# A hybrid decoder step on one core: head norms summed in two column groups, roots by Ln and Exp, halves carried by DMA

## The reference, cut to what matters

```python
def rmsnorm(x, g):
    return x * rsqrt(mean(x * x) + EPS) * g                  # over D_MODEL = 1024
def group_rmsnorm(o, g):
    return o * rsqrt(mean(o * o over one head) + EPS) * g    # over 128 features of one head

n = rmsnorm(x, ln1)
rq, rk, rv, rg, gq, gk, gv, gg, ga, m_r, m_g = split_cols(n @ w_in)
o_r = retention of rotary(rq), rotary(rk), rv                # 4 heads, dk 128, dv 128
y_r = (group_rmsnorm(o_r, g_ret) * silu(rg)) @ w_ret_out
o_g = gated linear attention of gq, gk, gv, ga               # 4 heads, dk 64, dv 128
y_g = (group_rmsnorm(o_g, g_gla) * silu(gg)) @ w_gla_out
x = x + (sigmoid(m_r) * y_r + sigmoid(m_g) * y_g) @ w_o
...                                                          # rmsnorm ln2, ConvFFN of width 2816, final norm
```

## Time and profile before

| | us |
|---|---|
| median of three runs | 824.88 |
| lowest, highest | 824.02, 825.15 |
| the profiled execution | 826.43 |
| span of its trace (first to last instruction) | 824.60 |
| mean granted clock of PE | 0.997 of full speed |

### The profile page before, as it was taken

How to read it: one execution, slowest core, us unless ns; L and a number is a source line. 1 busy time by engine, 2 the same in 40 slices (tenths; PEclk the granted TensorE clock), 3 DMA queues, 4 the chain that set the end, 5 groups by cost and what they waited for, 6 DMA issues and landing times.

```text
span 824.6 us, 15722 instructions
## 1 busy us (share of the span) xinstructions
PE 815.2 (99%) x6528; PEld 801.7 (97%) x6528; DVE 587.9 (71%) x765; ACT 376.4 (46%) x528; POOL 217.0 (26%) x258
## 2 busy tenths in 40 slices
PE   9999999999999999999999999999999999999996
PEld 9999999999989999999999999999999999999996
DVE  4465768487899877766558877777777756778973
ACT  5554234332456363543344544444444424544574
POOL 4018246443427400000530333333222322000020
PEclk9999999999999999999999999999999999999998
DMA  8769978983327973547996687576677874765622
GB/s 270 220 204 152 252 228 189 204 248 115 127 77 137 213 243 115 179 137 234 189 275 199 124 261 217 142 203 191 246 190 204 230 171 102 200 181 172 174 63 108
DMA packets 163025, 152.29 MB, mean 185 GB/s; under 512 B 6677, under 2 KB 144617, under 8 KB 162940
## 3 DMA queue, kind: packets, MB, share of 16 engines
q1 hardware_dynamic: 129420, 109.73, 42.8%
q0 software_dynamic: 33376, 41.05, 26.6%
q10 hardware_dynamic: 160, 0.53, 0.2%
HBM read 145.32 MB, written 58.40 MB: 247 GB/s over the span
## 4 chain that ended last, share of the span: by engine, by line
PE 96%; DVE 3%; issue 0%; ACT 0%; DVEq 0%
PE mm L2050 52%; PE ax L2356 14%; PE mm L2470 8%; PE ax L2470 6%; PE ax L2069 6%; PE mm L2356 4%; PE ax L2074 3%; PE mm L2131 1%; PE mm L2069 1%; DVE grs L1469 1%; PE mm L2062 0%; DVE ysil L1712 0%; DVE ylo L1717 0%; DVE wlo L1729 0%; DVE wlo L1459 0%
## 5 line engine op out<-in xcount | busy, mean ns | idle before, releaser
L2050 PE MATMUL mm<-nhi,whi 128*128 128x272 f32 x928 | 196.2, 293 | 0.0
L2050 PE MATMUL mm<-nhi,wlo 128*128 128x272 f32 x928 | 191.9, 288 | 0.0
L2050 PE MATMUL mm<-nlo,whi 128*128 128x272 f32 x928 | 191.4, 288 | 0.0
L1027 ACT ACTIVATE whi<-raw 128x1024 fp32r<-128x1024 f32 (+3 forms) x112 | 128.5, 1181 | 64.8 <-PE mm L2050 34.7
L2050 PEld LDWEIGHTS mm<-nhi,whi 128*128 128x128 f32 x928 | 146.2, 188 | 2.9 <-issue 1.1
L2050 PEld LDWEIGHTS mm<-nlo,whi 128*128 128x128 f32 x928 | 145.8, 188 | 0.0
L2050 PEld LDWEIGHTS mm<-nhi,wlo 128*128 128x128 f32 x928 | 145.0, 189 | 0.0
L1729 DVE TENSOR_TENSOR wlo<-raw,whi 128x1024 fp32r<-128x1024 f32 (+1 forms) x78 | 84.4, 1123 | 5.9 <-ACT whi L1027 3.5
L1459 DVE TENSOR_TENSOR wlo<-raw,whi 128x2048 fp32r<-128x2048 f32 x27 | 65.2, 2414 | 14.7 <-ACT whi L1027 14.6
L958 POOL DMA_DIRECT2D v_sums<-in_w_up x24 | 30.7, 4230 | 117.4 <-DVE mlo L1800 115.8
L1027 ACT ACTIVATE whi<-ring 128x1408 fp32r<-128x1408 f32 x25 | 34.6, 1383 | 44.1 <-PE ax L2470 24.0
(11 more groups left out here) (393 smaller groups left out, 1979.4 us busy)
## 6 DMA issues: line engine op xcount, KB each, us to landing
raw<-in_w_in SPq DMA_DIRECT2D x36, 512.0 KB, 5.2
raw<-in_w_up SPq DMA_DIRECT2D x36, 512.0 KB, 7.0
ring<-w_sums SPq DMA_DIRECT2D x16, 704.0 KB, 4.9
w_sums<-in_w_down SPq DMA_DIRECT2D x9, 768.0 KB, 10.5
w_sums<-in_w_down POOLq DMA_DIRECT2D x9, 768.0 KB, 9.5
ring<-in_w_down SPq DMA_DIRECT2D x9, 704.0 KB, 4.6
v_sums<-in_w_up SPq DMA_DIRECT2D x24, 256.0 KB, 7.8
v_sums<-in_w_up POOLq DMA_DIRECT2D x24, 256.0 KB, 14.7
```

The lines of the kernel that those rows point to most:

```text
L1027: return act.activation(out, in_, func, **kw).then_inc(done, 1)
L2050: ins = pe.matmul(mm[:, 2 * j + a, 0:HALF], w, x[:, kx, HALF * a:HALF * (a + 1)], start=first and n == 0 and m == 0, stop=last and n == le ...
```

## The change

The seven norms gn0 to gn3 and rn0 to rn2 are done in another way; rn3 keeps the sums over whole rows. For the seven, PE multiplies 64 columns of ones (`ones[:, 0:GLA_DK]`) by each half of the tokens, the first half into partitions 0 to 63 and the second into partitions 64 to 127 (`PAIR`) of one bank, so that the two halves stand one above the other in 272 columns. ACT takes Ln of sum/128 + eps from the bank into a tile `logs` (128x272), then Exp of -0.5 times that twice, 64 partitions each, into the root tile: partitions 0 to 63 get the first half of tokens, 64 to 127 the second. What is missing, each half on the other 64 partitions, is carried by two SBUF to SBUF transfers issued from ACT's queue (64 partitions x 1088 bytes = 68 KB each). DVE waits for these (`root_in`) and has no reciprocal. For rn3 ACT takes Ln of 544 columns and Exp in place, and DVE waits for that (`root_ready`). rstd1 and rstd2 get Ln and Exp on ACT in place of Sqrt on ACT and reciprocal on DVE.

In the order, gi 2 moves from (12,0)@4 to (12,1)@4, gi 3 from there to (13,0)@4, ri 0 from behind (13,0) to (13,1)@4, ri 1 from there to (14,0)@4, ri 2 from (14,1)@4 to behind (14,1) and sl 7, and ri 3 from ahead of y2 5 to behind y1 6. gi 0 and gi 1 stay. The lines that allocate `logs` and the new semaphores are left out here.

```diff
@@ -168,10 +168,10 @@
-        (13, 0): [("rs", 2), ("rp", 2), ("ri", 0), ("y1", 2)],
+        (13, 0): [("rs", 2), ("rp", 2), ("y1", 2)],
-        (14, 1): [("rn", 3), ("sl", 6), ("sl", 7), ("ri", 3), ("y2", 5), ("y1", 6), ("y1", 7), ("y2", 6), ("y2", 7)],
+        (14, 1): [("rn", 3), ("sl", 6), ("sl", 7), ("ri", 2), ("y2", 5), ("y1", 6), ("ri", 3), ("y1", 7), ("y2", 6), ("y2", 7)],
@@ -179,12 +179,12 @@
-        (11, 1): {2: [("v", 7)], 4: [("ro", 0)]}, (12, 0): {4: [("gn", 2), ("rk", 1), ("gsq", 3), ("gi", 2)]},
-        (12, 1): {4: [("rs", 1), ("rp", 1), ("gi", 3)]},
-        (13, 0): {4: [("rx", 1), ("rw", 1)], 5: [("rk", 2)], 6: [("rn", 0), ("rsq", 1)]},
-        (13, 1): {4: [("rn", 1), ("ri", 1), ("y2", 0)]},
-        (14, 0): {4: [("rx", 2), ("rw", 2), ("rsq", 2)], 5: [("rk", 3)]},
-        (14, 1): {1: [("rs", 3)], 2: [("rp", 3)], 4: [("rn", 2), ("ro", 3), ("ri", 2)], 6: [("rx", 3), ("rw", 3), ("rsq", 3), ("y1", 5), ("y2", 4)]},
+        (11, 1): {2: [("v", 7)], 4: [("ro", 0)]}, (12, 0): {4: [("gn", 2), ("rk", 1), ("gsq", 3)]},
+        (12, 1): {4: [("rs", 1), ("rp", 1), ("gi", 2)]},
+        (13, 0): {4: [("rx", 1), ("rw", 1), ("gi", 3)], 5: [("rk", 2)], 6: [("rn", 0), ("rsq", 1)]},
+        (13, 1): {4: [("rn", 1), ("ri", 0), ("y2", 0)]},
+        (14, 0): {4: [("rx", 2), ("rw", 2), ("rsq", 2), ("ri", 1)], 5: [("rk", 3)]},
+        (14, 1): {1: [("rs", 3)], 2: [("rp", 3)], 4: [("rn", 2), ("ro", 3)], 6: [("rx", 3), ("rw", 3), ("rsq", 3), ("y1", 5), ("y2", 4)]},
@@ -1048,10 +1051,12 @@
 
         squares = [0]
 
-        def root(name, width):
+        def inverse_root(name, width):
 
             aux_wait_filled(act, name)
-            run(halves(rstd[:, :]), bank2(name), ACT.Sqrt, drained_sem(name), scale=1.0 / width, bias=eps)
+            run(halves(rstd[:, :]), bank2(name), ACT.Ln, drained_sem(name), scale=1.0 / width, bias=eps)
+            aux_wait_drained(act, name)
+            run(rstd[:, :], rstd[:, :], ACT.Exp, rstd_ready, scale=-0.5)
 
         def first_high(c):
 
@@ -1097,7 +1102,7 @@
                 act.wait_ge(filled[j], fills(j, u))
                 run(halves(gqk[:, 2 * u + j, :]), slot(j), ACT.Copy, drained[j])
             elif k == "rstd1":
-                root("rstd1", D_MODEL)
+                inverse_root("rstd1", D_MODEL)
             elif k == "v":
                 aux_wait_filled(act, s)
                 big, small = vdst(s[1])
@@ -1160,9 +1165,22 @@
                 run(gsq[:, :], normed(NORMS[n]), ACT.Square, osq_done)
             elif k in ("gn", "rn"):
                 aux_wait_filled(act, s)
+                i = norms % 2
+                log, root = logs[k == "rn"], grs2[i]
                 if norms > 1:
                     act.wait_ge(o_ready, norms - 1)
-                run(halves(grs2[norms % 2][:, :]), bank2(s), ACT.Sqrt, drained_sem(s), scale=1.0 / DV, bias=eps)
+                if s == NORMS[-1]:
+                    run(halves(root[:, :]), bank2(s), ACT.Ln, drained_sem(s), scale=1.0 / DV, bias=eps)
+                    aux_wait_drained(act, s)
+                    run(root[:, :], root[:, :], ACT.Exp, root_ready, scale=-0.5)
+                    continue
+                run(log[:, :], bank(s, 0)[:, 0:HALF], ACT.Ln, drained_sem(s), scale=1.0 / DV, bias=eps)
+                aux_wait_drained(act, s)
+                for r, t in zip(PAIR, HALVES):
+                    run(root[r, t], log[r, :], ACT.Exp, root_ready, scale=-0.5)
+                act.wait_ge(root_ready, 2 * (norms + 1))
+                for a in range(2):
+                    act.dma_start(root[PAIR[1 - a], HALVES[a]], root[PAIR[a], HALVES[a]]).then_inc(root_in[i], 16)
                 norms += 1
             elif k == "rope":
                 i = s[1]
@@ -1302,7 +1320,7 @@
                     for k in range(4):
                         run(tile(usum[0], k), resid[:, k, HALVES[1]], ACT.Copy, t_first, scale=vec(V_LN2 + k))
             hi(u + 2, u % 2, 32 * (u // 2 + 2), (filled[1], FW[1] + n + 1))
-        root("rstd2", D_MODEL)
+        inverse_root("rstd2", D_MODEL)
 
         for i in range(KF // 2):
             x, b = up_unit(i), up_block(i)
@@ -1464,10 +1482,6 @@
             dve.wait_ge(filled[j], count)
             dve.tensor_tensor(halves(out), slot(j), halves(rstd[:, :]), ALU.mult).then_inc(drained[j], 1)
 
-        def inverse(out, name, done):
-            aux_wait_drained(dve, name)
-            dve.reciprocal(out, out).then_inc(done, 1)
-
         adds = [0]
 
         def add_square(out, places, first):
@@ -1530,7 +1544,6 @@
                 st.wait()
                 dve.tensor_tensor(acc[:, :], sq8[:, 0, :], sq8[:, 1, :], ALU.add).then_inc(acc1_done, 1)
             elif k == "rstd1":
-                inverse(rstd[:, :], "rstd1", rstd_ready)
                 dve.wait_ge(rstd_ready, 1)
             elif k == "sc":
                 for j in range(2):
@@ -1645,9 +1658,10 @@
             elif k in ("gi", "ri"):
                 s = ("gn" if k == "gi" else "rn", s[1])
                 root = grs2[norms % 2]
-                inverse(root[:, :], s, dve_step)
-                st.n += 1
-                st.wait()
+                if s == NORMS[-1]:
+                    dve.wait_ge(root_ready, 2 * len(NORMS) - 1)
+                else:
+                    dve.wait_ge(root_in[norms % 2], 32 * (norms // 2 + 1))
                 h = s[1]
                 norms += 1
                 dve.scalar_tensor_tensor(normed(s), normed(s), vec((V_GGLA if k == "gi" else V_GRET) + h), root[:, :],
@@ -1843,7 +1857,7 @@
                 if f >= 5:
                     make_sums(usum, V_LN2, f - 5)
             lo(u + 2, u % 2, u + 3)
-        inverse(rstd[:, :], "rstd2", rstd_ready)
+        aux_wait_drained(dve, "rstd2")
         dve.memset(ext[:, 0:2], 0.0).then_inc(conv_done, 1)
         dve.wait_ge(rstd_ready, 2)
         for i in range(2):
@@ -2296,7 +2310,12 @@
                           done=filled_sem(s) if a else None)
             elif k in ("gn", "rn"):
                 pe.wait_ge(osq_done, NORMS.index(s) + 1)
-                summed(s, gsq)
+                if s == NORMS[-1]:
+                    summed(s, gsq)
+                    continue
+                aux_take(pe, s)
+                for r, t in zip(PAIR, HALVES):
+                    small(bank(s, 0)[r, 0:HALF], ones[:, 0:GLA_DK], gsq[:, t], done=filled_sem(s) if r is PAIR[1] else None)
             elif k == "rk":
                 pe.wait_ge(qk_ready, 8)
                 turn_tokens(s, qk[:, HEADS + s[1], :])
```

More of the change, by code:

```diff
@@ L306, in build @@
     hsq = [sqt, gsq]
+    logs = [at(f"logs{k}", [P, HALF], C + o4) for k, o4 in enumerate((8 * T, 10 * T + 2 * DV * 4))]
+    assert 2 * DV * 4 + HALF * 4 <= T
     grs2 = [grs, at("grs1", [P, NT], C + 11 * T)]
@@ L432, in build @@
     sq_done, acc_done = sem("sq_done"), sem("acc_done")
-    rstd_ready = sem("rstd_ready")
+    rstd_ready, root_ready = sem("rstd_ready"), sem("root_ready")
+    root_in = [sem(f"root_in{i}") for i in range(2)]
     last_sq, last_sums, last_roots, last_rstd = map(sem, ("last_sq", "last_sums", "last_roots", "last_rstd"))
```

## The result

The change made the kernel slower: 827.72 us, the median of 8 runs (826.28 to 828.55), against 824.80 for the kernel before (8 runs): ratio 1.0029, 95% interval 1.0019 to 1.0039. (That ratio is the estimate on record; the two medians alone give 1.0035.) The forecast was 824.6 us and no change, its range ended at 827.1. The profiled execution after took 828.55 us with a span of 826.7.

What follows compares the result with a forecast made beforehand. PE, busy for 99% of the span, was taken as the bound. Terms -1.21 - 1.17 + 0.7 + 0.2 + 1.2 = -0.28 took the profiled 826.43 to 826.15; less 1.55 to the median, 824.6 us, range 822.4 to 827.1.

Steps and rivals of the forecast that it cites:

- Part 2: DVE's queue ahead of rs3 and rn2: with the reciprocals gone, rss is no longer late for PE, -1.17 us.
- Part 3: ACT's roots, 3.4 us per norm: gsq3 late for PE at gn3, +0.7; other steps behind a root, +0.2 together.
- Part 1: PE's sums in column groups: 0.13 us saved on each of six, 0.43 at rn2; -1.21 us together.
- Rival A: Column groups on PE run fully side by side: -3.3 us instead of -1.21, 822.5 us; chance 0.15.
- Part 5: Last norm, rn3: ACT's loads delay DVE's gsig, so PE's product that needs it comes later, +1.2 us.
- Part 4: Moved multiplications and carrying DMAs: landings covered by the half unit, nought; without the cover at most 1.17 us.
- Part 6: rstd1 and rstd2: each loses a 3.5 us DVE reciprocal, gets an Exp and perhaps two loads; nought.
- B: No load on ACT between Ln and Exp: gn3's 0.7 and the tail's 1.2 vanish, 822.7 us; chance 0.07.
- C: DMA issues hold ACT, 0.8 us each, deciding from about 0.75: +2.1 us, 826.7 us; chance 0.13.
- D: The column groups on PE do not overlap: +1.3 us instead of -1.21, 827.1 us; chance 0.10.

Runs made afterwards that it cites:

- e2: Changed kernel with gi2, gi3, ri0 and ri1 back at their former places; ratio 1.0012 against the kernel before.
- e8: Changed kernel, arithmetic untouched, reordered: gn2's and rn2's Exp and carry later, gi3, ri0, ri1 back, two Silu and two low parts later; 823.67 us, ratio 0.9975.
- e12: Changed kernel with gi3 alone moved half a unit back, behind gi2; one execution, 120.29 us from ahead of the first norm to gate unit 16.
- e1: Changed kernel with all eight norms whole, no column groups and no carrying DMA; ratio 1.0018 against the kernel before.
- e7: Changed kernel with copies in place of Ln and Exp in all eight head norms, so no loads between them; ratio 1.0000 against the kernel before.
- e11: Whole-row kernel e1 with ri1 alone moved half a unit back; one execution, 118.67 us from ahead of the first norm to gate unit 16.
- e5: Changed kernel with copies in place of Ln and Exp in the last norm, rn3, only; ratio 1.0002 against the kernel before.
- e4: Changed kernel with Exp and carry as a step of their own, later in ACT's queue, rn1 staying; ratio 1.0012 against the kernel before.

## Why the prediction was wrong, by its steps

The sum was -0.28 and came out at +2.05, 2.33 more. Of that rn2 has 0.91, rk3 and ro3 together 0.48, gn3 0.40, gate unit 16 0.26, rs2 0.25 and gn1 0.13; rs3 was 0.10 better. The largest failure is one step, which the prediction put as "With 7 us gone from this queue ... rss is no longer late: -1.17".

**Part 2, DVE's late queue.** rs3 gave its gain; rn2 gave 0.39 of the 1.30 that parts 1 and 2 had there together, and rs2 lost 0.25. It was not the landings, which the prediction named as the way to nothing: DVE's waits for them, up to 3.89 us, cost nothing in e2 and e8. It was two things that it looked past. The moved multiplications came to stand ahead of the retention's steps (e2, and e12 for gi3), and DVE's ylo waited for ACT's yhi. "One multiplication of 0.79 moved by half a unit within it" was priced by its duration alone: ri1 still took 0.78 in the changed kernel, but ahead of rk3's keys it made rss late (without the moves, in e2, the first wait at rn2 is gone), gi3 took 1.45 beside POOL's rvm, and where ri1 met rvm (e1, e7) it took 3.37 (e11 shows it for e1). That the reciprocals held DVE was right: with whole sums, no reciprocals and ri1 put back (e11), rs3 and rn2 gave -1.38, where the forecast had 1.17 as the most. With gi3, ri0 and ri1 put back and ACT's late steps moved out as well (e8), they gave -1.70, what parts 1 and 2 had for these two, to a tenth. The reciprocals were not DVE's only load, though: y1's multiplication beside rvm (2.44 before, 0.72 otherwise) had 1.72 us of the queue ahead of rss, more than the 0.87 that PE waited at rn2. By this estimate a move of that one step might have bought the same; no run tested it in the kernel before.

**Part 3, the roots on ACT.** The mechanism at gn3 was right, its size was not: 3.95 us for 3.4, of which the two issues had 0.34 (1.12 for 0.78), Ln 0.09 and the two Exp 0.08, and PE lost 0.97 there with its sum for 0.57. The "+0.2 together" for the others was wrong in kind: I asked what stands directly behind a root. rn1's root delays what comes behind the next eight instructions: ACT has hardly any idle time from 226.90 on through yhi, split, rso, load, three Silu and another yhi, and rx2's copy is 0.53 late for PE. With two of the Silu behind it (e8) that loss is gone.

**Part 1, the sums.** The size was right where PE comes from products (0.09 to 0.16 measured, 0.13 forecast). gn1 gave nothing, since PE waits for DVE's rks right behind it. Rival A is out: a sum of two groups takes 0.61 us from start to start, not 0.46. The two halves do start together, 0.01 us apart by the single records; but an fp32 sum has two products per half, and from one pair to the next it is 0.28 us and from the second pair to what follows 0.33, where a product at full width takes 0.23. The Trainium skill (TensorE: Matmul & The Clock Gate, "Part 3: Packing small matmuls") has a pack last as one product; the trace differs by 0.15.

**Part 5, the last norm.** Right as a mechanism and nearly in size (1.46 for 1.2, which left out the 0.14 from the end of DVE's gsig to PE's start); e5 shows the loads as its cause. What the prediction missed is how cheaply it is cured.

**Parts 4 and 6.** Part 4 was right on the landings: the carries landed in 3.5 us (median of 14) and no landing cost PE time. The moves, which it put at nought, cost 0.56 (e2). Part 6 held: the two other roots cost nothing.

**Rivals.** B is out: there is a load of 1.28 us between Ln and Exp in every norm (e7 shows what the norms' loads are worth, 2.38 of stretch). C was right in direction and half in mechanism: an issue took 0.56 in the changed kernel, under its point of 0.75, yet the pair held ACT nearly as long as the load, and without the issues (e1) gn3 lost 0.04. D is out: a sum takes 0.61, not more than 0.92. The range failed because it took the bad ends of the steps one at a time; nearly all that went wrong went the same way, most of it for one reason: the queues of two engines were taken as free because they were not the bound. The miss beyond its end is small: 824.80 and the stretch's 2.05 make 826.85, inside it, and the median lies 0.6 above it.

## What to carry to other kernels

Before work is moved to an engine that is "not the bound", follow that engine's queue from the new work to its next idle time, and ask of every instruction in between who waits for it; here that would have shown rk3 and DVE's ylo. Before an instruction is moved along its queue, look at what other engines do at its new place, since its duration may not come along. And where an engine reaches a step late, look for work ahead of it that nobody needs yet: moving two Silu, two Exp and two low parts, with three multiplications put back, turned 1.0029 into 0.9975.

## What was not expected of the hardware

- **DVE beside POOL.** The same multiplication took 0.78 us alone, 1.45 beside part of POOL's rvm (gi3), and 3.37 beside rvm and what followed it (ri1, in e1); ylo took 2.21 instead of 0.72. Each of these ended 0.58 or 0.59 us after POOL's instruction (ylo at 239.44, rvm at 238.86), as if it had run behind it; in e8 ylo came through in 0.72 and rvm took 2.51 instead of 1.90. DVE's s0r, which reads one of its inputs from PSUM, took 1.22 beside rvm (e1) and 1.21 without. Why ri1 lasted past rqd, which began 0.88 us after rvm's end, stays open. The Trainium skill (GPSIMD Engine Reference, "1. Specifications") says that POOL shares its SBUF interfaces with VectorE, with contention for DVE instructions that have two SBUF inputs; the slowed ones have two, s0r has one, and the trace agrees.
- **Issues in a pair.** Two DMA issues in a row on ACT's queue took 1.12 us at most places, but 1.59 and 1.80 at two in e7 and 1.76 at one in e4, where the single one took 0.39.
